# Last expert of an encoder layer: four tile squares moved among its gate and up steps, epsilon and row sums moved to ScalarE, row additions moved between VectorE's tile scalings

## The chip, the cores and the metric

The kernel runs on one core of a Trainium2 chip. The metric is the device time of one execution in microseconds (us), lower is better; the median of several runs is compared. TensorE does the matrix products, VectorE (DVE in the rows) and ScalarE (ACT) do the elementwise work, GpSimd (POOL) issues gathers and scatters and does some small arithmetic, and SyncE (SP) issues most transfers. Each engine works through its own instructions in order; a wait on a semaphore holds back everything behind it on that engine.

## The reference, cut to what matters

One encoder layer: attention of two kinds, an output projection, a mixture of 16 experts and a final norm. 1536 tokens (1024 of a prompt, 512 of a sample) of width 1024, fp32. The change touches the last expert and the final norm:

```python
def expert_choice_moe(x, w_router, w_gate, w_up, w_down):
    ...
    gate, idx = lax.top_k(aff.T, cap)          # each expert picks 128 prompt and 64 sample tokens
    xg = xt[idx]
    h = jax.nn.silu(jnp.einsum('ecd,edf->ecf', xg, w_gate)) * jnp.einsum('ecd,edf->ecf', xg, w_up)
    y = jnp.einsum('ecf,efd->ecd', h, w_down) * gate[..., None].astype(x.dtype)
    out = jnp.zeros_like(xt).at[idx.reshape(-1)].add(y.reshape(-1, D))
...
x = x + expert_choice_moe(rmsnorm(x, norm2), ...)
return rmsnorm(x, final_norm)                  # x * rsqrt(mean(x * x) + eps) * final_norm
```

## The kernel before

Experts run one after the other. For one expert, TensorE computes eight column blocks f = 0 to 7 of the gate and up products (16 pairs of matmuls each, L1969 and L1971), then two output halves c = 0 and 1 of the down product (40 matmuls each, L1988 to L1992). All weights come as fp32 and are used as two rounded parts: ScalarE makes the rounded part (`split_rounded`, L1838, two instructions for one unit) and VectorE the rest (`split_rest`, L1652, two instructions for one unit). An expert has 12 such units: 0 to 7 hold gate and up, 8 to 11 hold down. TensorE starts block f only when the units of that block are split (f = 6 needs unit 7) and when the sums of block f - 2 are out of PSUM.

ScalarE's and VectorE's work of an expert is written as steps z = 0 to 15. In steps 1 to 7 ScalarE does, in this order: `move` (copy block z - 1 of gate and up out of PSUM, L1843 and L1844), `split_rounded` of unit z + 2 (L1838), `silu` (L1861), `round_hidden` (L1865). VectorE does `sums` (L1658, L1661), `split_rest` of unit z + 2 (L1652), `hidden` (L1667) and `hidden_rest` of block z - 2 (L1674). `round_hidden` waits for `hidden`; the next `move` waits for `hidden_rest`. Unit 10 is split in step 8, unit 11 in step 10.

The final norm of the 12 row tiles (128 rows each) is woven into the last expert. After the expert before it has added its rows to x2 in DRAM, SyncE loads tiles 0 to 2 into `own_rows` (L1534) and signals them, with `final_weight`, on `final_loaded[0]`; once units 0 to 7 are split it loads tiles 3 to 10 into the free weight buffers, and once unit 9 is split, tile 11. ScalarE squares and sums each tile (`final_square`, L1870), GpSimd adds epsilon and takes the root of three tiles together (`final_roots`, L1601 and L1604), VectorE scales the tile (`final_scale`, L1714), SyncE stores it (L1549). The rows that the last expert itself changes are done apart: VectorE adds the down product to them (`finish_rows`, L1725 to L1731, one call for each output half), for which ScalarE first scales a part (`scale_output`, `y_rest`, L1851); ScalarE squares them (`row_square`, L1880), GpSimd takes their roots (L1610 to L1616), VectorE scales them (`finish_scale`, L1736), and GpSimd scatters them over the stored tiles (L1633). That scatter waits for all 12 tile stores (`final_stored`) and is the last thing the program does.

The step in which a tile is squared or scaled comes from two tables, `SQUARES_IN_STEP` and `FINAL_IN_STEP`; the order on each engine is otherwise that of the code.

Of the kernel before, what the change touches and what calls it, by code (L numbers as in the profile page):

```python
# [24 lines left out]
ALU = mybir.AluOpType  # L25
# [1303 lines left out]
def experts(p):  # L1329
# [35 lines left out]
    SQUARES_IN_STEP = {8: (0,), 9: (1, 2), 10: (3,), 11: (4, 5), 12: (6, 7), 13: (8, 9), 14: (10, 11)}  # L1365
    FINAL_IN_STEP = {9: (0,), 10: (1, 2), 11: (3, 4), 12: (5,), 13: (6, 7, 8), 14: (9, 10, 11)}
    with ExitStack() as st:
# [65 lines left out]
        final_stored = sem("final_stored")  # L1433
        base_gathered = sem("base_gathered")
# [3 lines left out]
        row_eps_added = sem("row_eps_added")  # L1438
        row_rstd = sem("row_rstd")
# [75 lines left out]
        with nc.Block() as block:  # L1515
# [37 lines left out]
            def _(pool):  # L1553
# [38 lines left out]
                pool.memset(flip[:, :], 0.0).then_inc(flip_ready, 1)  # L1592
                pool.wait_ge(flip_ready, 1)
# [4 lines left out]
                def final_roots(group):  # L1598
                    ts = slice(FINAL_GROUP * group, FINAL_GROUP * (group + 1))
                    pool.wait_ge(final_squared, ts.stop)  # L1600
                    pool.tensor_tensor(final_stats[:, 0, ts], final_stats[:, 0, ts],  # L1601
                                       p.d_eps[:, :].broadcast_to([P, FINAL_GROUP]), ALU.add).then_inc(final_eps_added, 1)
                    pool.wait_ge(final_eps_added, group + 1)
                    pool.tensor_tensor(final_stats[:, 1, ts], final_stats[:, 0, ts],  # L1604
                                       p.minus_half[:, :].broadcast_to([P, FINAL_GROUP]), ALU.pow
                                       ).then_inc(final_rstd, 1)

                def row_root(g, n):
                    pool.wait_ge(row_squared, 3 + g)
                    pool.tensor_tensor(fix_stats[0:n, g, 0:1], fix_stats[0:n, g, 0:1], p.d_eps[0:n, :], ALU.add  # L1610
                                       ).then_inc(row_eps_added, 1)
                    pool.wait_ge(row_eps_added, 2 * g + 1)
                    pool.tensor_tensor(fix_stats[0:n, g, 2:3], fix_stats[0:n, g, 0:1], fix_stats[0:n, g, 1:2], ALU.add
                                       ).then_inc(row_eps_added, 1)
                    pool.wait_ge(row_eps_added, 2 * g + 2)
                    pool.tensor_tensor(fix_stats[0:n, g, 3:4], fix_stats[0:n, g, 2:3], p.minus_half[0:n, :], ALU.pow  # L1616
                                       ).then_inc(row_rstd, 1)

                def finish():
# [8 lines left out]
                    for g, n in enumerate((CAP_P, CAP_S)):  # L1628
                        row_root(g, n)
# [16 lines left out]
            def _(dve):  # L1646
# [86 lines left out]
                def finish_scale(g):  # L1733
                    y, n = ((y_p, CAP_P), (y_s, CAP_S))[g]
                    dve.wait_ge(row_rstd, g + 1)
# [47 lines left out]
                def step(x):  # L1783
                    for z in range(16):
# [23 lines left out]
                        if z == 14 and x.is_last:  # L1808
                            finish_rows(x, 0)
                        if z == 9 and x.is_last:  # L1810
# [7 lines left out]
                    if x.is_last:  # L1818
                        finish_rows(x, 1)
                        for g in range(2):  # L1820
# [5 lines left out]
            def _(act):  # L1826
# [45 lines left out]

                def row_square(g, c):

                    cs = slice(c * 512, (c + 1) * 512)
                    y, n = ((y_p, CAP_P), (y_s, CAP_S))[g]
                    act.wait_ge(row_done, 2 * c + g + 1)
# [12 lines left out]
                def step(x):  # L1890
                    for z in range(16):
# [10 lines left out]
                        if 1 <= z <= 7:  # L1902
                            silu(x.e, z - 1)
                            round_hidden(x.e, z - 1)
# [5 lines left out]
                        if x.is_last:  # L1910
                            for t in SQUARES_IN_STEP.get(z, ()):
                                final_square(t)
                    if x.is_last:
                        for g in range(2):
                            row_square(g, 0)
                        scale_output(x, 1)
                        for g in range(2):
                            row_square(g, 1)

# [197 lines left out]
```

## Time and profile before

| | us |
|---|---|
| median of 3 runs (1816.41 to 1817.06) | 1816.84 |
| the profiled execution, its own time | 1817.82 |
| its span, in which all rows lie | 1816.0 |

The profiled execution is 0.98 us above the median. A time in a row counts from the start of the span. In a timeline row stand start, duration, engine, line, operation, what it writes and reads, the number of instructions, and in brackets the idle time before it with what ended it. SPq is the queue of transfers that SyncE issues. PEclk is the granted clock of TensorE, 1.00 for 2.4 GHz and 0.50 for 1.2 GHz.

### The profile page before, as it was taken

What the parts mean: (1) busy time and instruction counts of PE and PEld (TensorE: products, weight loads), DVE (VectorE), ACT (ScalarE), POOL (GpSimd) and SP (SyncE); (2) the same over time, 40 slices, a digit from 0 to 9 for tenths busy, and PEclk for the clock granted to TensorE, in tenths of its full rate; (3) what the DMA queues carried; (4) which work ended last, traced back from release to release, by engine and by line L of the source; (5) the groups of instructions that cost most, each with busy time, mean ns of one, the idle gap of its engine ahead of it and who ended that gap; (6) DMA issues with size and microseconds to landing.
All of it is one profiled execution on the core that took longest, in us unless ns stands there. A gap on an engine that the chain in (4) does not pass through costs nothing.

```text
span 1816.0 us, 30873 instructions
## 1 busy us (share of the span) xinstructions
PE 1716.9 (95%) x10662; PEld 1570.6 (86%) x10662; DVE 1188.6 (65%) x2313; ACT 1031.5 (57%) x2031; POOL 409.1 (23%) x563
## 2 busy tenths in 40 slices
PE   6999999899999989997599999999999999999994
PEld 6789798689999978886499999999999999999993
DVE  4442433277777864327778777787777877778776
ACT  4433333278888982111367666676666666666665
POOL 1222302244445542221101111001110011100113
PEclk9999999899999999998699999999999999999997
DMA  7455636554444744333767777777777787776784
GB/s 231 122 170 181 185 111 154 150 156 144 148 142 132 204 112 143 111 108 123 266 224 254 260 249 261 245 257 260 243 248 249 248 266 254 231 263 243 258 291 189
DMA packets 203609, 367.08 MB, mean 202 GB/s; under 512 B 39183, under 2 KB 64783, under 8 KB 202959
## 3 DMA queue, kind: packets, MB, share of 16 engines
q1 hardware_dynamic: 190268, 320.92, 52.5%
q0 software_dynamic: 13248, 44.96, 9.5%
q8 instruction: 53, 0.87, 0.2%
q14 instruction: 40, 0.33, 0.1%
HBM read 321.67 MB, written 50.45 MB: 205 GB/s over the span
## 4 chain that ended last, share of the span: by engine, by line
PE 47%; DVE 3%; ACT 1%; POOL 1%; issue 0%; DMA 0%; DVEq 0%; ACTq 0%; POOLq 0%
PE psum L1969 21%; PE psum L1971 10%; PE psum L1988 3%; PE psum L1990 3%; PE psum L1992 3%; PE psum L1989 3%; PE psum L1991 3%; DVE weight_parts L1652 1%; PE psum L1955 1%; DVE raw_weights L1714 1%; PE psum L1952 1%; ACT weight_parts L1838 0%; DVE top_at L1308 0%; DVE affT L1310 0%; ACT xT_e L1870 0%
## 5 line engine op out<-in xcount | busy, mean ns | idle before, releaser
L1969 PE MATMUL psum<-x_parts,weight_parts 128*128 128x384 f32 x2048 | 586.0, 360 | 2.0 <-DVE x_parts L1701 2.0
L1971 PE MATMUL psum<-x_parts,weight_parts 128*128 128x192 f32 x2048 | 513.8, 251 | 0.0
L1652 DVE TENSOR_TENSOR weight_parts<-raw_weights,weight_parts 128x1024 fp32r<-128x1024 f32 x384 | 451.5, 1221 | 69.5 <-ACT weight_parts L1838 69.5
L1838 ACT ACTIVATE weight_parts<-raw_weights 128x1024 fp32r<-128x1024 f32 x384 | 382.3, 1055 | 27.9 <-PE psum L1992 16.3
L1971 PEld LDWEIGHTS psum<-x_parts,weight_parts 128*128 128x128 f32 x2048 | 392.5, 192 | 0.6
L1969 PEld LDWEIGHTS psum<-x_parts,weight_parts 128*128 128x128 f32 x2048 | 385.8, 188 | 2.8 <-DVE x_parts L1701 2.2
L552 PE MATMUL psum<-x_hi,w_parts 128*128 128x512 f32 x624 | 193.9, 390 | 1.6 <-DVE kS L419 1.6
L1589 POOL DMA_INDIRECT x<-y_p,index x15 | 24.1, 1608 | 637.4 <-DVE y_s L1709 637.4
L1865 ACT ACTIVATE h_parts<-up_sum 128x192 fp32r<-128x192 f32 x128 | 46.7, 365 | 173.7 <-DVE up_sum L1667 173.7
L1143 PE MATMUL psum<-w_o_parts,mixed_parts 128*128 128x512 f32 x576 | 139.7, 399 | 4.3 <-DVE w_o_parts L1234 4.3
L779 POOL TENSOR_TENSOR logits_da<-logits_da 128x512 f32<-128x512 f32 (+1 forms) x96 | 103.8, 1103 | 171.7 <-DVE logits_da L863 171.7
L552 PEld LDWEIGHTS psum<-x_hi,w_parts 128*128 128x128 f32 x624 | 117.1, 188 | 28.9 <-issue 4.6
L1143 PEld LDWEIGHTS psum<-w_o_parts,mixed_parts 128*128 128x128 f32 x576 | 108.5, 191 | 26.9 <-issue 4.5
L552 PE MATMUL psum<-x_lo,w_parts 128*128 128x512 f32 x312 | 121.5, 389 | 0.0
L905 ACT ACTIVATE logits_da<-logits_da,stats 128x1024 f32<-128x1024 f32 (+1 forms) x96 | 96.0, 1001 | 41.0 <-DVE stats L831 40.4
L827 DVE CUSTOM_DVE_ANT_0 logits_da<-psum,bias_da 128x1024 f32<-128x1024 f32 (+1 forms) x96 | 96.9, 1044 | 33.9 <-PE psum L961 27.3
L1658 DVE TENSOR_TENSOR gate_sum<-psum,gate_sum 128x192 f32<-128x192 f32 x128 | 45.8, 358 | 103.4 <-ACT gate_sum L1843 103.4
L376 DVE TENSOR_TENSOR w_parts<-mixed,w_parts 128x2048 fp32r<-128x2048 f32 (+1 forms) x30 | 62.4, 2078 | 70.1 <-ACT w_parts L476 70.1
L329 POOL DMA_DIRECT2D q<-mixed x96 | 59.7, 628 | 200.9 <-DVE mixed L408 200.0
L1988 PE MATMUL psum<-weight_parts,h_parts 128*128 128x512 f32 x256 | 101.4, 396 | 0.3 <-DVE h_parts L1674 0.3
L1990 PE MATMUL psum<-weight_parts,h_parts 128*128 128x512 f32 x256 | 99.7, 390 | 0.0
L1992 PE MATMUL psum<-weight_parts,h_parts 128*128 128x512 f32 x256 | 99.7, 389 | 0.0
(207 smaller groups left out, 3103.5 us busy)
## 6 DMA issues: line engine op xcount, KB each, us to landing
raw_weights<-in_w_gate SPq DMA_DIRECT2D x32, 2048.0 KB, 7.8
raw_weights<-in_w_up SPq DMA_DIRECT2D x32, 2048.0 KB
raw_weights<-in_w_down SPq DMA_DIRECT2D x32, 2048.0 KB, 7.8
mixed<-in_w_in SPq DMA_DIRECT2D x96, 256.0 KB, 4.2
q_parts<-q SPq DMA_DIRECT2D x192, 128.0 KB, 3.0
bias_da<-da_rows SPq DMA_DIRECT2D x32, 512.0 KB, 4.2
q<-mixed POOLq DMA_DIRECT2D x96, 128.0 KB, 3.0
mixed<-in_x SPq DMA_DIRECT2D x12, 512.0 KB, 5.8
```

What stands on the lines that cost most here:

```text
L552: mm = pe.matmul(out, lhsT(kt), rhs(kt), start=(kt == 0 and i == 0), stop=(kt == KT - 1 and i == len(passes) - 1))
L779: pool.tensor_tensor(logits_da[:, it.slot, 0, cs], logits_da[:, it.slot, 0, cs], logits_da[:, it.slot, 1, cs], ALU.add).then_inc(combined, 1)
L827: dve.tensor_tensor_reduce(out, bank(p, 2 * m, width), bias, 1.0, -3.0e38, ALU.add, ALU.max, col(it, "max", 1, m)).then_inc(logits_ready, 1)
L905: act.activation(out, src, ACT.Exp, bias=col(it, "negmax", 1, m), accum_out=col(it, "sum", 1, m)).then_inc(exp_done, 1)
L1143: mm = pe.matmul(bank(p, 2 * i + c), mixed_parts[:, i, a, j, :], w_parts[:, b, j, c * 512:(c + 1) * 512], start=(j == 0 and k == 0), stop= ...
L1652: dve.tensor_tensor(part_half(u, 1, half), src, part_half(u, 0, half).bitcast(F32), ALU.subtract).then_inc(split, 1)
L1838: act.activation(part_half(u, 0, half), src, ACT.Copy).then_inc(rounded, 1)
L1969: pe.matmul(out.rearrange("p (h n) -> p h n", h=2), w[:, 0, k, cols], x_parts[:, k, :, :], start=(k == 0), stop=False)
L1971: mm = pe.matmul(out[:, 0:SLOTS], w[:, 1, k, cols], x_parts[:, k, 0, :], start=False, stop=(k == KT - 1))
L1988: pe.matmul(down_bank(0, c), h_hi, w_hi[:, n, :], start=first, stop=False)
L1990: pe.matmul(down_bank(0, c), h_lo, w_hi[:, n, :], start=False, stop=last)
L1992: mm = pe.matmul(down_bank(1, c), h_sample, w_lo[:, n, :], start=False, stop=last)
```

## The change

Four tiles are squared in steps 4 to 7 (`EARLY_SQUARES`), each between `silu` and `round_hidden`; the other eight follow in steps 8, 11 and 12. Tile 0 is scaled in step 7, tiles 1 and 2 in step 8, 3 to 5 in step 11, 6 to 8 in step 14, and 9 to 11 after the last `finish_rows`. The first `finish_rows` stands in step 12, ahead of tiles 6 to 8. The scaling of `final_weight` goes from step 9 to step 6. Epsilon is added by ScalarE, once for three tiles and once for the rows; the rows' two halves are summed by ScalarE too, and GpSimd takes one root for both groups of rows; it clears `fix_stats` at the start of the expert part.

```diff
-    SQUARES_IN_STEP = {8: (0,), 9: (1, 2), 10: (3,), 11: (4, 5), 12: (6, 7), 13: (8, 9), 14: (10, 11)}
-    FINAL_IN_STEP = {9: (0,), 10: (1, 2), 11: (3, 4), 12: (5,), 13: (6, 7, 8), 14: (9, 10, 11)}
+    EARLY_SQUARES = {4: (0,), 5: (1,), 6: (2,), 7: (3,)}
+    SQUARES_IN_STEP = {8: (4, 5), 11: (6, 7, 8), 12: (9, 10, 11)}
+    FINAL_IN_STEP = {7: (0,), 8: (1, 2), 11: (3, 4, 5), 14: (6, 7, 8)}
+    FINAL_AFTER = (9, 10, 11)
...
+                pool.memset(fix_stats[:, :, :], 0.0).then_inc(fix_cleared, 1)
...
-                    pool.wait_ge(final_squared, ts.stop)
-                    pool.tensor_tensor(final_stats[:, 0, ts], final_stats[:, 0, ts],
-                                       p.d_eps[:, :].broadcast_to([P, FINAL_GROUP]), ALU.add).then_inc(final_eps_added, 1)
...
+                def row_roots():
+                    pool.wait_ge(row_summed, 2)
+                    pool.tensor_tensor(fix_stats[:, :, 3], fix_stats[:, :, 2], p.minus_half[:, :].broadcast_to([P, 2]),
+                                       ALU.pow).then_inc(row_rstd, 1)
...
-                        if z == 14 and x.is_last:
+                        if z == 12 and x.is_last:
                             finish_rows(x, 0)
-                        if z == 9 and x.is_last:
+                        if z == 6 and x.is_last:
                             dve.wait_ge(final_loaded[0], 16 * 4)
...
                     if x.is_last:
                         finish_rows(x, 1)
+                        for t in FINAL_AFTER:
+                            final_scale(t)
                         for g in range(2):
                             finish_scale(g)
...
+                def add_final_eps(group):
+                    ts = slice(FINAL_GROUP * group, FINAL_GROUP * (group + 1))
+                    act.wait_ge(final_squared, ts.stop)
+                    act.activation(final_stats[:, 0, ts], final_stats[:, 0, ts], ACT.Identity, bias=p.d_eps[:, :]
+                                   ).then_inc(final_eps_added, 1)
...
                             silu(x.e, z - 1)
+                            if x.is_last:
+                                for t in EARLY_SQUARES.get(z, ()):
+                                    final_square(t)
+                                    if t % FINAL_GROUP == FINAL_GROUP - 1:
+                                        add_final_eps(t // FINAL_GROUP)
                             round_hidden(x.e, z - 1)
...
                         scale_output(x, 1)
+                        add_row_eps()
                         for g in range(2):
                             row_square(g, 1)
+                            sum_row_squares(g)
```

On ScalarE, step 4 of the last expert (the names are tiles; `own_rows` is a row tile, `h_parts` the rounded hidden block), before:

```order
L1838 ACTIVATE weight_parts<-raw_weights 128x1024 [waits gate_up,raw_loaded0]
L1838 ACTIVATE weight_parts<-raw_weights 128x1024
L1861 ACTIVATE gate_sum<-gate_sum 128x192 [waits gate_summed]
L1865 ACTIVATE h_parts<-up_sum 128x192 [waits h_done]
L1843 ACTIVATE gate_sum<-psum 128x192 [waits h_split,gate_up]
```

The same place in the change:

```order
L1835 ACTIVATE weight_parts<-raw_weights 128x1024 [waits gate_up,raw_loaded0]
L1835 ACTIVATE weight_parts<-raw_weights 128x1024
L1858 ACTIVATE gate_sum<-gate_sum 128x192 [waits gate_summed]
L1867 ACTIVATE xT_e,final_stats<-own_rows 128x1024 [waits final_loaded0]
L1862 ACTIVATE h_parts<-up_sum 128x192 [waits h_done]
L1840 ACTIVATE gate_sum<-psum 128x192 [waits h_split,gate_up]
```

The square of tile 0 with its wait for `final_loaded[0]` now stands ahead of `round_hidden` of step 4 and of the `move` of step 5.

On ScalarE, steps 8 to 14 of the last expert, before (`y_rest` is `scale_output`):

```order
L1838 ACTIVATE weight_parts<-raw_weights 128x1024 [waits gate_up,raw_loaded3]
L1838 ACTIVATE weight_parts<-raw_weights 128x1024
L1870 ACTIVATE xT_e,final_stats<-raw_weights 128x1024 [waits final_squared,final_loaded1] x3
L1870 ACTIVATE xT_e,final_stats<-raw_weights 128x1024 [waits final_squared,final_loaded2] x3
L1870 ACTIVATE xT_e,final_stats<-raw_weights 128x1024 [waits final_squared,final_loaded3]
L1851 ACTIVATE y_rest<-psum,gate 64x512 [waits y_ready_s,down]
L1870 ACTIVATE xT_e,final_stats<-raw_weights 128x1024 [waits final_squared,final_loaded3] x2
```

In the change, from unit 10 on:

```order
L1867 ACTIVATE xT_e,final_stats<-raw_weights 128x1024 [waits final_squared,final_loaded1] x2
L1873 ACTIVATE final_stats<-final_stats,d_eps 128x3 [waits final_squared]
L1835 ACTIVATE weight_parts<-raw_weights 128x1024 [waits gate_up,raw_loaded3]
L1835 ACTIVATE weight_parts<-raw_weights 128x1024
L1867 ACTIVATE xT_e,final_stats<-raw_weights 128x1024 [waits final_squared,final_loaded2] x3
L1873 ACTIVATE final_stats<-final_stats,d_eps 128x3 [waits final_squared]
L1867 ACTIVATE xT_e,final_stats<-raw_weights 128x1024 [waits final_squared,final_loaded3] x3
L1873 ACTIVATE final_stats<-final_stats,d_eps 128x3 [waits final_squared]
L1848 ACTIVATE y_rest<-psum,gate 64x512 [waits y_ready_s,down]
```

`scale_output` of half 0 now stands behind all twelve squares and three additions of epsilon.

On VectorE, the end of the program, before:

```order
L1725 SCALAR_TENSOR_TENSOR y_p<-psum,gate,rows_p 128x512 [waits down]
L1727 SCALAR_TENSOR_TENSOR y_s<-psum,gate,rows_s 64x512
L1731 TENSOR_TENSOR y_s<-y_s,y_rest 64x512 [waits y_rest_moved,sample_added]
L1736 SCALAR_TENSOR_TENSOR y_p<-y_p,fix_stats,final_weight 128x1024 [waits row_rstd]
L1736 SCALAR_TENSOR_TENSOR y_s<-y_s,fix_stats,final_weight 64x1024 [waits row_rstd]
```

In the change:

```order
L1720 SCALAR_TENSOR_TENSOR y_p<-psum,gate,rows_p 128x512 [waits down]
L1722 SCALAR_TENSOR_TENSOR y_s<-psum,gate,rows_s 64x512
L1726 TENSOR_TENSOR y_s<-y_s,y_rest 64x512 [waits y_rest_moved,sample_added]
L1709 SCALAR_TENSOR_TENSOR raw_weights<-raw_weights,final_stats,final_weight 128x1024 [waits final_rstd] x3
L1731 SCALAR_TENSOR_TENSOR y_p<-y_p,fix_stats,final_weight 128x1024 [waits row_rstd]
L1731 SCALAR_TENSOR_TENSOR y_s<-y_s,fix_stats,final_weight 64x1024 [waits row_rstd]
```

The last three tiles are scaled behind the rows' last additions, and ahead of the rows' scaling.

## Rows read from the trace of the kernel before

**Rows 1.** Page, first lines: the span, instructions

```profile
span 1816.0 us, 30873 instructions
```

**Rows 2.** Chain of work that ended last: start, duration, engine, tile, line

```profile
1800.66 0.60 POOL fix_stats L1610
...
1804.36 2.03 POOL y L1633
```

**Rows 3.** Timeline of ScalarE, steps 4 to 8 of the last expert

```profile
1754.87 0.36 ACT L1861 ACTIVATE gate_sum<-gate_sum 128x192 f32<-128x192 f32 x1
1756.73 0.36 ACT L1865 ACTIVATE h_parts<-up_sum 128x192 fp32r<-128x192 f32 x1 [1.50 <-DVE up_sum L1667]
1757.13 0.33 ACT L1843 ACTIVATE gate_sum<-psum 128x192 f32<-128x192 f32 x1
...
1766.31 0.33 ACT L1843 ACTIVATE gate_sum<-psum 128x192 f32<-128x192 f32 x1
...
1772.71 1.99 ACT L1838 ACTIVATE weight_parts<-raw_weights 128x1024 fp32r<-128x1024 f32 x2
```

**Rows 4.** Timeline of ScalarE, squares of the row tiles

```profile
1774.61 1.05 ACT L1870 ACTIVATE xT_e<-own_rows 128x1024 f32<-128x1024 f32 x1
1775.56 0.18 ACT L1870 ACTIVATION_READ_ACCUMULATOR xT_e<-own_rows 128x1 f32 x1
1775.84 1.06 ACT L1870 ACTIVATE xT_e<-own_rows 128x1024 f32<-128x1024 f32 x1
```

**Rows 5.** Load of tile 2: issue, microseconds to landing; then stretches, last columns PEclk, DMA share, GB/s

```profile
1746.24 0.48 SPq L1534 DMA_DIRECT2D own_rows<-x  x1
own_rows<-x SPq DMA_DIRECT2D x1, 512.0 KB, 14.6
1758.00:1758.50 0.50, 0.50 (x6) 0.50 (x5) 0.11 (x1) 0.50 (x1) 0.00 (x0) 1.00 0.89 352
1760.00:1760.50 0.50, 0.50 (x6) 0.50 (x5) 0.50 (x1) 0.00 (x0) 0.00 (x0) 1.00 0.04 16
```

**Rows 6.** Timeline of VectorE: split of unit 7, then the tail; then the tile stores' landing

```profile
1758.66 2.36 DVE L1652 TENSOR_TENSOR weight_parts<-raw_weights,weight_parts 128x1024 fp32r<-128x1024 f32 x2 [0.55 <-ACT weight_parts L1838]
...
1794.89 0.68 DVE L1731 TENSOR_TENSOR y_s<-y_s,y_rest 64x512 f32<-64x512 f32 x1
1795.51 3.66 DVE L1714 SCALAR_TENSOR_TENSOR raw_weights<-raw_weights,final_stats,final_weight 128x1024 f32<-128x1024 f32 x3
1799.09 0.73 DVE L1725 SCALAR_TENSOR_TENSOR y_p<-psum,gate,rows_p 128x512 f32<-128x512 f32 x1
...
1800.52 0.68 DVE L1731 TENSOR_TENSOR y_s<-y_s,y_rest 64x512 f32<-64x512 f32 x1
...
y<-raw_weights SPq DMA_DIRECT2D x9, 512.0 KB, 2.8
```

**Rows 7.** Timeline of TensorE: block 0, down product's ends, an earlier phase

```profile
1734.08 0.33 PE L1969 MATMUL psum<-x_parts,weight_parts 128*128 128x384 f32 x1
...
1770.95 0.47 PE L1988 MATMUL psum<-weight_parts,h_parts 128*128 128x512 f32 x1 [0.33 <-DVE h_parts L1674]
...
1788.98 0.39 PE L1992 MATMUL psum<-weight_parts,h_parts 128*128 128x512 f32 x1
...
680.25 19.47 PE L1143 MATMUL psum<-w_o_parts,mixed_parts 128*128 128x512 f32 x72 [4.35 <-DVE w_o_parts L1234]
```

**Rows 8.** Stretches: length, busy time of PE, PEld, DVE, ACT, POOL, then PEclk, DMA

```profile
681.00:686.00 5.00, 5.00 (x14) 3.84 (x13) 5.00 (x5) 4.40 (x5) 2.53 (x1) 0.50 1.13 220
687.00:688.00 1.00, 1.00 (x6) 0.78 (x6) 1.00 (x2) 0.96 (x1) 0.00 (x0) 1.00 1.06 414
...
889.00:894.00 5.00, 4.81 (x18) 4.81 (x19) 3.27 (x4) 1.77 (x2) 1.47 (x2) 0.50 0.63 170
894.00:895.00 1.00, 1.00 (x7) 1.00 (x6) 0.00 (x0) 0.00 (x0) 0.00 (x0) 0.72 0.76 268
236.00:238.00 2.00, 0.90 (x7) 0.90 (x8) 1.97 (x5) 0.00 (x0) 0.00 (x0) 1.00 0.10 9
```

More of the change, by code:

```diff
@@ L1433, in experts @@
         final_stored = sem("final_stored")
+        fix_cleared = sem("fix_cleared")
         base_gathered = sem("base_gathered")
@@ L1438, in experts @@
         row_eps_added = sem("row_eps_added")
+        row_summed = sem("row_summed")
         row_rstd = sem("row_rstd")
@@ L1606, in final_roots @@
                                        ).then_inc(final_rstd, 1)
[L1608 to L1617, printed above, removed]
+                def row_roots():
+                    pool.wait_ge(row_summed, 2)
+                    pool.tensor_tensor(fix_stats[:, :, 3], fix_stats[:, :, 2], p.minus_half[:, :].broadcast_to([P, 2]),
+                                       ALU.pow).then_inc(row_rstd, 1)
                 def finish():
@@ L1627, in finish @@
                         final_roots(group)
-                    for g, n in enumerate((CAP_P, CAP_S)):
-                        row_root(g, n)
+                    row_roots()
                     pool.wait_ge(final_stored, 16 * TILES)
@@ L1734, in finish_scale @@
                     y, n = ((y_p, CAP_P), (y_s, CAP_S))[g]
-                    dve.wait_ge(row_rstd, g + 1)
+                    dve.wait_ge(row_rstd, 1)
                     dve.scalar_tensor_tensor(y[:, :], y[:, :], fix_stats[0:n, g, 3:4], final_weight[0:n, :],
@@ L1871, in final_square, with add_row_eps, sum_row_squares @@
                                    ).then_inc(final_squared, 1)
+                def add_final_eps(group):
[3 more added lines that the diff above has]
+                                   ).then_inc(final_eps_added, 1)
+                def add_row_eps():
+                    act.wait_ge(row_squared, 2)
+                    act.activation(fix_stats[:, :, 0], fix_stats[:, :, 0], ACT.Identity, bias=p.d_eps[:, :]
+                                   ).then_inc(row_eps_added, 1)
+                def sum_row_squares(g):
+                    act.wait_ge(row_eps_added, 1)
+                    act.wait_ge(row_squared, 3 + g)
+                    act.activation(fix_stats[:, g, 2:3], fix_stats[:, g, 1:2], ACT.Identity, bias=fix_stats[:, g, 0:1]
+                                   ).then_inc(row_summed, 1)
                 def row_square(g, c):
@@ L1876, in row_square @@
                     y, n = ((y_p, CAP_P), (y_s, CAP_S))[g]
+                    act.wait_ge(fix_cleared, 1)
                     act.wait_ge(row_done, 2 * c + g + 1)
@@ L1912, in step @@
                                 final_square(t)
+                                if t % FINAL_GROUP == FINAL_GROUP - 1:
+                                    add_final_eps(t // FINAL_GROUP)
                     if x.is_last:
```

## The prediction

> **What bounds the kernel now.** I read the chain of work that ended last first [rows 2]: from about 1780 us on it runs through VectorE's tile scalings and row additions, then GpSimd's roots, and ends with GpSimd's scatter, which starts at 1804.36. What lies behind that start (the second scatter, its landing, the end of the program) the change leaves alone, so the question is when the scatter starts. Of the span of 1816.0 us [rows 1] the change can only touch the last expert, from 1734.08 [rows 7]. Second comes ScalarE's timeline of the gate and up steps [rows 3], because that is where the change puts new work; third the time at which that work's data arrive [rows 5]; fourth who waits for ScalarE there: VectorE [rows 6] and TensorE [rows 7, 8].
>
> TensorE's block f takes (1770.95 - 0.33 - 1734.08) / 8 = 4.57 us, some 0.02 of it drain, so 4.55 [rows 7]. ScalarE's steps come every 4.59 us (1757.13 to 1766.31 is two) [rows 3]. The two are level: nothing that holds ScalarE for more than a step stays hidden from TensorE.
>
> **The room in a step.** `silu` of step 4 starts at 1754.87 and ends at 1755.23; `round_hidden` waits 1.50 us for VectorE until 1756.73 [rows 3]. A square lasts 1.13 us, from 1774.61 to the end of its accumulator read, 1775.56 + 0.18 [rows 4]. So with its data in place an early square fits into the wait and costs nothing; the addition of epsilon in step 6 (a ScalarE instruction on 128x3, not in the trace; between the 0.18 of the accumulator read [rows 4] and the 0.36 of a 128x192 one [rows 3], I take 0.25, near the smaller form) takes the rest of it, 0.12 us at most beyond it. That was the easy half.
>
> **Its data are not in place.** Tiles 0 to 2 signal one semaphore, and the square of tile 0 waits for all. The load of tile 2 is issued at 1746.24 and lands 14.6 us later, at 1760.84, behind the last weights: the transfer engines are 0.89 busy at 1758 and at 0.04 in 1760.0 to 1760.5 [rows 5]. Before, nobody read these tiles before 1774.61 [rows 4]. Now ScalarE stands from 1755.2 to 1760.84, 5.6 us, with `round_hidden` of step 4 and the next `move` behind it. Square (1.13) and `round_hidden` (0.36) put that `move` at 1762.33 against 1757.13: 5.2 us late. Behind it in a row wait ScalarE's split of unit 7, VectorE's half of that split, `hidden` and all later steps. SyncE's loads of tiles 3 to 10 wait for unit 7 too and shift with it; the squares that read them shift as much, so that costs nothing more.
>
> **TensorE.** The split of unit 7 ended at 1758.66 + 2.36 = 1761.02 [rows 6]; now at 1766.2. Block 6 needs it and could start at 1734.08 + 6 x 4.55 = 1761.4. TensorE idles 4.8 us, where before it did not idle in these steps. After an idle of 4.35 us earlier in the program its clock was at 0.50 (1.2 GHz) from 681 to 686 and at 1.00 (2.4 GHz) from 687 [rows 7, 8]. This very pair of matmuls, at 0.50 in 889 to 894, took 4.81 / 9 = 0.534 us a pair against 4.55 / 16 = 0.284, and the low level lasted about 0.56 us into the next one [rows 8], some 10 pairs: 10 x 0.25 = 2.5 us. I take that for block 6: it ends at 1766.2 + 4.55 + 2.5 = 1773.3, and ScalarE's `move` of it starts 0.2 later, at 1773.5 against 1766.31 [rows 3]: 7.2 us late. Had the clock stayed up, it would be ScalarE's own 5.2.
>
> The page "TensorE: Matmul & The Clock Gate" of the Trainium skill, "HAM oscillation", says that a wait for data that is long enough throttles the array and the next work starts cold; Part 1 adds that the moment varies from run to run. By that rule, with which the 4.35 us gap agrees, the time is the forecast's; without it, it is that of the second rival.
>
> **The tail.** The first split of unit 10 started at 1772.71 [rows 3]. Now it is 7.2 later, and 1.1 more: VectorE scales tile 0 in step 7, ahead of the sums of block 7 for which `silu` waits (3.66 / 3 = 1.22 us [rows 6], less 0.1 in which it waited anyway). So it starts at 1781.0. Behind it ScalarE has until `y_rest`: two units, 1.90 each (1772.71 to 1774.61 [rows 3, 4]) = 3.8; eight squares of 1.23 (1774.61 to 1775.84 [rows 4]) = 9.8; three additions of epsilon = 0.75; 14.4 in all. `y_rest` starts at 1795.4, lasts 0.68, and VectorE adds it at 1796.1 instead of 1794.89 [rows 6]. Here ScalarE, not VectorE, is late, so the stall reaches the end.
> From that addition the three scalings and the next `finish_rows` follow as before: 1799.09 - 1794.89 = 4.20 gives 1800.3; the `finish_rows` itself, 1800.52 - 1799.09 + 0.62 = 2.05, ends at 1802.35; three more scalings, 3.66, end at 1806.0 [rows 6]. The last store is issued 0.1 later, lands 2.8 us after [rows 6], at 1808.9, and the scatter follows 0.2 later at 1809.1 against 1804.36: **4.7 us later**.
>
> **What costs or gives nothing.** GpSimd's row roots stood in the chain from 1800.66 until the scatter, 3.7 us [rows 2]. In the change they run beside VectorE's last three scalings, and so do ScalarE's three small additions of the rows: about 1803 to 1804.5, ahead of 1806. That is the gain meant for the tail, and it is real: without the stall all is 7.2 earlier, the scatter 2.5 us earlier than before. The rows' scalings (two of 1.28) lie beside the last store's landing. TensorE's last matmul ended at 1789.4 [rows 7] and now ends 7.2 later, at 1796.6; VectorE comes to its second half at 1800.3, so 3.7 us of cover remain. The scaling of `final_weight` (one pass over 128x1024, bounded by a tile scaling's 1.22) stands in step 6, where VectorE waits 0.55 for ScalarE's split [rows 6] and where block 6, 2.0 later than ScalarE, sets the pace. The memset of GpSimd stands at the start of the expert part, far ahead of its use.
>
> **The sum.** 1816.0 + 4.7 = 1820.7 for the span. The profiled execution was at 1817.82, 0.98 above the median; the difference lies outside what I move, so I add to the median: 1816.84 + 4.7 = **1821.5 us**.
>
> **Rivals.** (1) **The stall does not come** because tiles 0 to 2 are in place at 1755.2: the early squares are free, and 4.7 - 7.2 = -2.5 gives 1814.3, faster. It decides at once: every us that they land after 1755.2 is one us at the end, and the clock's fall adds 2 where TensorE's idle brings it about. Against it stand 14.6 us of landing and the busy engines [rows 5]; for it, nothing. 6%. (2) **The clock stays at 2.4 GHz** through the idle: 4.7 - 2.0 = 2.7, 1819.5. For it: in 236 to 238 TensorE was idle for 1.10 of 2.00 us and kept 1.00 [rows 8]. That idle is far shorter than 4.8. 12%. (3) **The landing is earlier** by up to 1.8 us, since only a trickle moves after 1759: 2.9 or more, from 1819.7. 12%. (4) **The change moves nothing at the end**, because the tail has more slack than I give it, VectorE and not ScalarE setting the `y_rest` addition: then it falls due near 1794.9 and the new order costs the three scalings behind the second `finish_rows`, minus the roots no longer in the way: within 3 us, 1818 to 1819.5. 4%.
>
> **How the numbers follow.** The forecast holds 66%. Its own spread: epsilon 0.18 to 0.36 three times, -0.2 to +0.3; the low clock as after 680.25, from there until between 686 and 687 [rows 7, 8], up to 6.7 us and thus up to 3.4 lost: +0.9; the landing, -1 to +0.5. Its own range is 1820.2 to 1822.9. The range reaches down to rivals 2 and 3: 1819.0 to 1823.0. A measurement of this kernel tells 0.2%, 3.6 us, from no change, so slower means over 1820.5. Slower: nearly all of the forecast, 65%. Same: rivals 2, 3, 4 and the forecast's lower edge, 28%. Faster: rival 1, and a little for what I do not see, 7%.
>
> **What the profile of the changed kernel would show.** ScalarE's first square at 1760.8 with an idle of over 5 us ahead of it, put down to a load; TensorE idle for some 4.8 us before a matmul of the gate and up blocks, with PEclk 0.50 for five to six us behind it; `y_rest` at about 1795.4; the last three scalings beside GpSimd's single root; the scatter at 1809, right behind the last store. The forecast is wrong if the first square starts by 1757, if no idle of TensorE stands in these steps, or if the last store lands before 1806.

## The result, and the profile of the changed kernel

The changed kernel takes 1820.93 us (median of 14 runs, 1819.06 to 1822.61), the kernel before beside it 1817.22 (14 runs, 1815.89 to 1818.91): a ratio of 1.0019 with the interval [1.0011, 1.0026], **3.7 us slower**. The forecast was 4.7 us slower, 1821.5. The profiled execution took 1820.95. Two executions among the experiments below, 5573.36 us in e7 and 4854.65 in e8, stand far outside all others and are left out of the medians and ratios.

The code ahead of the last expert is the same, but the executions do not reach it at the same moment: block 0 of the last expert starts at 1734.08 in the trace of before [rows 7] and at 1733.32 in that of after; over all traces below the moment varies from 1730.9 to 1735.0. So I count from block 0, in every kernel. The scatter started 70.28 us behind block 0 before [rows 2, 7], and 1808.43 - 1733.32 = 75.11 after it now: 4.83 later. The span ended 81.92 behind block 0 before [rows 1, 7], and ends 85.78 behind it now: 3.86 later. The second number is the one near the difference of the medians.

The page's first line, which answers to [rows 1]:

```profile
span 1819.1 us, 30877 instructions
```

Timeline of ScalarE (start, duration, engine, line, operation, and in brackets the idle time ahead with what ended it), for [rows 3, 4]:

```profile
1754.12 0.36 ACT L1858 ACTIVATE gate_sum<-gate_sum 128x192 f32<-128x192 f32 x1
1760.62 1.06 ACT L1867 ACTIVATE xT_e<-own_rows 128x1024 f32<-128x1024 f32 x1 [6.14 <-DMA own_rows<-x]
...
1761.68 0.34 ACT L1862 ACTIVATE h_parts<-up_sum 128x192 fp32r<-128x192 f32 x1
1761.93 0.31 ACT L1840 ACTIVATE gate_sum<-psum 128x192 f32<-128x192 f32 x1
...
1772.99 0.33 ACT L1840 ACTIVATE gate_sum<-psum 128x192 f32<-128x192 f32 x1 [1.94 <-PE psum L1995]
...
1794.62 0.69 ACT L1848 ACTIVATE y_rest<-psum,gate 64x512 f32<-64x512 f32 x1
```

`silu` of step 4 is over at 1754.48, and the square behind it waits 6.14 us for a load. `round_hidden` and the next `move` come out in a burst at 1761.68 and 1761.93; before, they stood at 1756.73 and 1757.13. The `move` at 1772.99 waits for TensorE, which none did in these steps before.

Timeline of TensorE and stretches of the same time (length, busy time and count of PE, PEld, DVE, ACT, POOL, then PEclk, DMA share, GB/s), for [rows 7, 8]:

```profile
1733.32 0.33 PE L1993 MATMUL psum<-x_parts,weight_parts 128*128 128x384 f32 x1
...
1765.85 0.69 PE L1993 MATMUL psum<-x_parts,weight_parts 128*128 128x384 f32 x1 [5.09 <-DVE weight_parts L1647]
```

```profile
1765.00:1770.00 5.00, 4.15 (x15) 4.15 (x16) 4.00 (x8) 4.50 (x9) 0.00 (x0) 0.50 0.60 221
1770.00:1771.00 1.00, 1.00 (x6) 1.00 (x6) 1.00 (x5) 0.83 (x4) 0.36 (x1) 0.61 0.87 344
1771.00:1773.00 2.00, 2.00 (x16) 2.00 (x15) 0.59 (x1) 0.06 (x2) 0.63 (x1) 1.00 1.02 397
```

TensorE stands for 5.09 us, where nothing stood before, and comes back at a granted clock of 0.50, its level of 1.2 GHz. Block 6 lasts from 1765.85 until the `move` behind it, 0.1 us earlier than 1772.99: about 7.03 us, against 4.55 before.

The tail: timelines of VectorE and GpSimd, and the last tile store (issue, then its landing), for [rows 2, 6]:

```profile
1795.41 0.68 DVE L1726 TENSOR_TENSOR y_s<-y_s,y_rest 64x512 f32<-64x512 f32 x1 [2.03 <-ACT y_rest L1848]
...
1801.64 3.66 DVE L1709 SCALAR_TENSOR_TENSOR raw_weights<-raw_weights,final_stats,final_weight 128x1024 f32<-128x1024 f32 x3
1805.90 1.28 DVE L1731 SCALAR_TENSOR_TENSOR y_p<-y_p,fix_stats,final_weight 128x1024 f32<-128x1024 f32 x1 [0.59 <-POOL fix_stats L1612]
1807.10 1.27 DVE L1731 SCALAR_TENSOR_TENSOR y_s<-y_s,fix_stats,final_weight 64x1024 f32<-64x1024 f32 x1
```

```profile
1802.99 2.88 POOL L1612 TENSOR_TENSOR fix_stats<-fix_stats,minus_half 128x2 f32<-128x2 f32 x1 [7.46 <-ACT fix_stats L1884]
1808.43 1.05 POOL L1628 DMA_INDIRECT y<-y_p,index  x1 [2.57 <-DVE y_s L1731]
```

```profile
1805.33 0.33 SPq L1553 DMA_DIRECT2D y<-raw_weights  x1
y<-raw_weights SPq DMA_DIRECT2D x1, 512.0 KB, 2.8
```

VectorE waits 2.03 us for `y_rest`; before, it did not. The last three scalings end at 1805.30, and the last store lands at 1805.33 + 2.8 = 1808.13. The scatter follows 0.30 later.

### The profile page after: what moved, and what is told of

The parts are those of the page before. It is cut to its first block, busy times and chain, and to the rows that moved or that the text cites. A ratio compares the mean times of both kernels' runs of the same rounds, so it can differ in the third digit from the quotient of the medians.

```text
span 1819.1 us, 30877 instructions
## 1 busy us (share of the span) xinstructions
PE 1719.0 (94%) x10662; PEld 1572.9 (86%) x10662; DVE 1188.1 (65%) x2313; ACT 1032.9 (57%) x2038; POOL 406.3 (22%) x555
## 4 chain that ended last, share of the span: by engine, by line
PE 49%; DVE 2%; ACT 1%; POOL 0%; issue 0%; DMA 0%; DVEq 0%; ACTq 0%
PE psum L1993 22%; PE psum L1995 10%; PE psum L2012 3%; PE psum L2014 3%; PE psum L2016 3%; PE psum L2013 3%; PE psum L2015 3%; PE psum L1979 1%; PE psum L1976 1%; ACT xT_e L1867 1%; DVE top_at L1308 0%; DVE affT L1310 0%; ACT weight_parts L1835 0%; DVE top L1306 0%; DMA rows_s<-xn,tokens 0%
```

## The experiments

Theory A is that of the prediction: the wait of the early square for its tile makes the stall, the stall makes TensorE's clock fall, and both reach the end through ScalarE. Theory B: the new order of the tail (rows added between the tile scalings, ScalarE's additions, one GpSimd root) costs the time. Theory C: the amount of work that ScalarE got into its gate and up steps costs it, wherever the data are. The two columns of starts and ends, and "against before", are from one trace of each kernel, counted from block 0; the medians and ratios are from runs beside the kernel before. e1 to e4 were timed beside 1816.37 (33 runs of before), e5 to e8 beside 1817.22 (30 runs). The ratios are recorded with their intervals and differ by up to 0.0003 from the plain quotient of two medians. Behind block 0 the traces of before and e2 agree within 0.01 us, but trace and medians differ by up to 1.4 us (e3: +1.64 and +3.05), so a difference smaller than that between two kernels rests on the traces alone.

| kernel | scatter starts behind block 0 | span ends behind block 0 | against before | median, ratio, interval |
|---|---|---|---|---|
| before | 70.28 | 81.92 | | |
| after | 75.11 | 85.78 | +3.86 | 1820.93, 1.0019 [1.0011, 1.0026] |
| e1 loads of own rows first | 67.66 | 78.41 | -3.51 | 1813.77, 0.9983 [0.9974, 0.9992] |
| e2 the same on before | 70.27 | 81.91 | -0.01 | 1816.43, 1.0001 [0.9992, 1.0010] |
| e3 TensorE kept busy | 72.85 | 83.56 | +1.64 | 1819.42, 1.0014 [1.0005, 1.0023] |
| e4 ScalarE's additions alone | 71.29 | 82.22 | +0.30 | 1816.99, 1.0001 [0.9992, 1.0010] |
| e5 early squares one step later | 68.46 | 79.16 | -2.76 | 1814.71, 0.9988 [0.9979, 0.9996] |
| e6 e1, `y_rest` earlier | 66.54 | 77.26 | -4.66 | 1812.09, 0.9970 [0.9958, 0.9981] |
| e7 e5, `y_rest` earlier | 66.99 | 77.67 | -4.25 | 1813.98, 0.9982 [0.9974, 0.9991] |
| e8 no early squares | 71.78 | 82.53 | +0.61 | 1817.92, 1.0003 [0.9994, 1.0012] |
| e9 e6, rows between the last tiles | 68.85 | 79.56 | -2.36 | one run each, 1815.39 beside 1816.59 |

**e1: the data in place.** On the change, SyncE issues the loads of tiles 0 to 2 ahead of the last `w_down` load, not behind it.

```diff
-                    for n, (name, half) in enumerate(LOADS):
+                    for n, (name, half) in enumerate(LOADS[:-1] if x.is_last else LOADS):
...
                 for t in range(OWN_ROWS):
                     load_final(t)
+                last = Expert(EXPERTS // 2 - 1, 1)
+                n = len(LOADS) - 1
+                name, half = LOADS[n]
+                ge(sp, split, 2 * (UNITS * last.e + LAST_UNIT[n - RAW] + 1))
+                slot = (len(LOADS) * last.i + n) % RAW
+                src = w_v[name][bass.ds(last.e, 1)].rearrange("a p k n -> p (a k) n")
+                sp.dma_start(raw[:, slot, :, :], src[:, :, half * 512:(half + 1) * 512]
+                             ).then_inc(loaded[slot], 16)
```

> The changed kernel, with one difference: SyncE issues the loads of tiles 0 to 2 and of final_weight ahead of the last expert's last 2 MB of down weights, not behind them. Theory (the early square of tile 0 waits for its load): the tiles land some 5 us earlier, near 1755.5; ScalarE's first square starts by 1755.8, TensorE does not idle in the gate and up blocks and its clock stays at 1.00; about 2.5 us faster than the kernel before (ratio near 0.9986), about 6 us faster than the change. Rival (the new order of the tail, or ScalarE's small additions, cost the time): no faster than the change, still 3 to 4 us slower than before.

The loads of the own rows now land 4.3 us behind their issue. Timelines of e1, ScalarE and VectorE:

```profile
1755.78 0.36 ACT L1866 ACTIVATE gate_sum<-gate_sum 128x192 f32<-128x192 f32 x1
1756.11 1.06 ACT L1875 ACTIVATE xT_e<-own_rows 128x1024 f32<-128x1024 f32 x1
...
1789.63 0.68 DVE L1734 TENSOR_TENSOR y_s<-y_s,y_rest 64x512 f32<-64x512 f32 x1 [2.03 <-ACT y_rest L1856]
```

The square starts at the end of `silu`, nothing waits, and TensorE does not idle in the gate and up blocks. The addition of `y_rest` comes 54.64 us behind block 0 instead of 62.09, the scatter 67.66 instead of 75.11: both 7.45 earlier, for all of the change's work is still there. Theories B and C fall: with the same order, the same instructions and the data in place, the changed kernel is 0.17% faster than the one before. VectorE waits 2.03 us for `y_rest` here too, so ScalarE is still the late one.

**e2: the same order of loads, on the kernel before.** The edit is that of e1.

> Control: the same exchange of loads in the kernel before. There the first square stands at 1774.6, after the landing at 1760.8 in any case. Theory: no change, within 0.5 us of before. Rival (the order of these loads is worth something by itself): more than 1 us faster.

Nothing: 1.0001, and the scatter at 70.27 against 70.28. What e1 gained is the wait taken away, not the loads' order.

**e3: the price of the clock.** On the change, TensorE multiplies 28 times more, into a bank that nobody reads, while it waits for unit 7. It adds work and leaves nothing out.

```diff
+                        if f == 6 and x.is_last:
+                            for i in range(28):
+                                pe.matmul(bank(p, 6, 2 * SLOTS).rearrange("p (h n) -> p h n", h=2),
+                                          x_parts[:, i % KT, 0, 0:P], x_parts[:, i % KT, :, :], start=True, stop=True)
                         if f % 2 == 0:
                             pe.wait_ge(split, 2 * (UNITS * x.e + u + 2))
```

> The changed kernel, with 28 matmuls of 384 columns into an unused PSUM bank ahead of block 6 of the last expert, where TensorE otherwise idles 5.1 us; their result is read by nobody. Theory: the idle is filled, the clock stays at 1.00 in block 6, ScalarE's move of block 6 is no longer 1.9 us late behind it, and the end comes about 2 us sooner: 1.7 us slower than before instead of 3.7. Rival (the low clock is hidden behind ScalarE): no difference from the change, 3.7 us slower than before. If the fillers outlast the wait, the gain shrinks by what they overrun.

Timelines and a stretch of e3:

```profile
1759.78 1.06 ACT L1867 ACTIVATE xT_e<-own_rows 128x1024 f32<-128x1024 f32 x1 [5.78 <-DMA own_rows<-x]
...
1760.12 5.07 PE L2026 MATMUL psum<-x_parts 128*128 128x384 f32 x28
1765.03 0.43 PE L1993 MATMUL psum<-x_parts,weight_parts 128*128 128x384 f32 x1
```

```profile
1766.00:1768.00 2.00, 2.00 (x17) 2.00 (x15) 1.43 (x3) 2.00 (x4) 0.00 (x0) 1.00 0.84 313
```

The wait of ScalarE is there as before (5.78 us), but TensorE goes on at 1.00. The `move` of block 6, which came 39.67 us behind block 0, comes 37.41 behind it (1770.25 - 1732.84), and the scatter 72.85: both 2.26 us earlier than in the change. Not all of that is the clock: in this execution the tiles landed sooner, and the first square started 26.94 us behind block 0 instead of 27.30. Block 6 started 0.34 us sooner too (32.19 against 32.53), before the clock could matter. So some 0.36 us of the 2.26 are the landing's, and 1.90 are the clock's; the change's ScalarE waited 1.94 us for TensorE at this `move`. The remaining 2.57 us (72.85 against 70.28) are the stall's own, less what the new tail gives.

The medians do not show this price as clearly: e3 is 3.05 us slower than the kernel before beside it, where 1.7 was expected, and the change 3.71, and the intervals of the two ratios overlap. The 1.90 us are read from the traces alone.

**e4: ScalarE's additions and the single root alone.** The squares, the scalings and the rows stand where they stood before; epsilon and the rows' sums are added by ScalarE.

```diff
-    EARLY_SQUARES = {4: (0,), 5: (1,), 6: (2,), 7: (3,)}
-    SQUARES_IN_STEP = {8: (4, 5), 11: (6, 7, 8), 12: (9, 10, 11)}
-    FINAL_IN_STEP = {7: (0,), 8: (1, 2), 11: (3, 4, 5), 14: (6, 7, 8)}
-    FINAL_AFTER = (9, 10, 11)
+    EARLY_SQUARES = {}
+    SQUARES_IN_STEP = {8: (0,), 9: (1, 2), 10: (3,), 11: (4, 5), 12: (6, 7), 13: (8, 9), 14: (10, 11)}
+    FINAL_IN_STEP = {9: (0,), 10: (1, 2), 11: (3, 4), 12: (5,), 13: (6, 7, 8), 14: (9, 10, 11)}
+    FINAL_AFTER = ()
...
-                        if z == 12 and x.is_last:
+                        if z == 14 and x.is_last:
                             finish_rows(x, 0)
-                        if z == 6 and x.is_last:
+                        if z == 9 and x.is_last:
```

> One part alone: ScalarE adds epsilon and the rows' sums and GpSimd takes one root for both groups of rows, with the tables and the order of the kernel before. Theory (the one root for both, 2.9 us in the trace of the change, is only free behind tile scalings): here nothing hides it, the rows' scalings start near 1805.5 instead of 1802.2, the scatter near 1807, so 2 to 3 us slower than before. Rival (fewer GpSimd instructions shorten the tail): 1 to 2 us faster than before.

It is level with before, 1.0001 [0.9992, 1.0010], where 2 to 3 us slower was expected. The end of e4, GpSimd and VectorE:

```profile
1801.82 0.70 POOL L1612 TENSOR_TENSOR fix_stats<-fix_stats,minus_half 128x2 f32<-128x2 f32 x1 [8.22 <-ACT fix_stats L1884]
1802.55 1.28 DVE L1731 SCALAR_TENSOR_TENSOR y_p<-y_p,fix_stats,final_weight 128x1024 f32<-128x1024 f32 x1 [2.00 <-POOL fix_stats L1612]
1803.76 1.27 DVE L1731 SCALAR_TENSOR_TENSOR y_s<-y_s,fix_stats,final_weight 64x1024 f32<-64x1024 f32 x1
1804.67 1.29 POOL L1628 DMA_INDIRECT y<-y_p,index  x1 [2.15 <-DVE y_p L1731]
```

The root, 2.88 us in the change, takes 0.70 here, and the scatter's issue 1.29 against 2.03 before. VectorE was idle beside the root and done early in the issue. So the row path of e4 is short enough to cost nothing, where it was expected to show. That is taken up below.

**e5: the early squares one step later**, so that the first comes when its tile has landed. The loads stay as in the change.

```diff
-    EARLY_SQUARES = {4: (0,), 5: (1,), 6: (2,), 7: (3,)}
-    SQUARES_IN_STEP = {8: (4, 5), 11: (6, 7, 8), 12: (9, 10, 11)}
-    FINAL_IN_STEP = {7: (0,), 8: (1, 2), 11: (3, 4, 5), 14: (6, 7, 8)}
+    EARLY_SQUARES = {5: (0,), 6: (1,), 7: (2,)}
+    SQUARES_IN_STEP = {8: (3, 4, 5), 11: (6, 7, 8), 12: (9, 10, 11)}
+    FINAL_IN_STEP = {8: (0, 1), 10: (2,), 11: (3, 4, 5), 14: (6, 7, 8)}
```

> The changed kernel with its early squares one step later: tiles 0, 1, 2 in steps 5, 6, 7, the other nine in steps 8, 11 and 12; tiles 0 and 1 scaled in step 8, tile 2 in step 10. The loads stand as in the change. Theory (only the wait of step 4's square for its load costs): the square of step 5 comes up near 1759.9 and waits about 1 us, most of it inside the 1.5 us that ScalarE waits there anyway; TensorE has no idle of note, its clock stays at 1.00, and the time is that of the first experiment, 2 to 3 us faster than before. Rival (early squares disturb the gate and up steps by themselves): 2 us or more slower than before.

The first square waits 1.13 us for the load instead of 6.14, starting 26.88 us behind block 0 (1761.12 - 1734.24; 27.30 in the change). TensorE does not idle in the gate and up blocks. The scatter comes at 68.46: 6.65 of e1's 7.45 us without touching a load. One step of 4.6 us was enough: the wait and the square (1.13 each) overrun the 1.50 us of room [rows 3], but the `move` behind them comes only 0.55 later than before (28.19 against 27.64 behind block 0). What e5 lacks to e1 is not that wait. Its first split of unit 10 starts earlier than e1's (39.17 against 39.61), but nine squares instead of eight stand between that split and `y_rest`, which starts at 54.65 against 53.86.

**e6: `y_rest` ahead of the last three squares**, with the edit of e1.

```diff
-                        if z == 14:
+                        if z == (12 if x.is_last else 14):
                             scale_output(x, 0)
```

> The first experiment's kernel (own rows loaded ahead of the last weights), and the first y_rest of ScalarE moved from behind the last three squares to before them (step 12). Theory (in the tail the change left VectorE waiting 2.0 us for y_rest): that wait goes, the last tile is scaled 2 us sooner and the end comes 1.5 to 2 us before the first experiment's, 4.5 to 5 us faster than before (ratio near 0.9973). Rival (something else ends last, such as the stores or the rows' root): no more than 0.5 us below the first experiment.

Timelines of e6, VectorE and GpSimd:

```profile
1781.43 3.67 DVE L1717 SCALAR_TENSOR_TENSOR raw_weights<-raw_weights,final_stats,final_weight 128x1024 f32<-128x1024 f32 x3 [0.75 <-POOL final_stats L1614]
...
1786.46 0.68 DVE L1734 TENSOR_TENSOR y_s<-y_s,y_rest 64x512 f32<-64x512 f32 x1
```

```profile
1777.26 4.14 POOL L1614 TENSOR_TENSOR final_stats<-final_stats,minus_half 128x3 f32<-128x3 f32 x1 [11.53 <-ACT final_stats L1881]
```

The wait of 2.03 us is gone. The scatter starts at 66.54, only 1.12 earlier than in e1, for a root of GpSimd took 4.14 us here and let VectorE wait 0.75 behind it (1.86 us and no wait in e1, at the same 44.3 us behind block 0). This is the fastest kernel here: 1812.09 (6 runs), **0.9970 [0.9958, 0.9981]** of the kernel before, 5.1 us faster than it and 8.8 faster than the change.

**e7: e5 and the earlier `y_rest`.** The edits of e5 and e6's, with the loads as in the change.

> Early squares from step 5 as in the fifth experiment, with the loads of the change, and y_rest ahead of the last three squares. Theory: it joins both gains without touching the loads, 3 to 4 us faster than before. Rival: as the fifth experiment.

In the trace the first square waits 0.47 us for its load, the scatter comes at 66.99 and the span ends 4.25 us earlier than before's. The median says less: 1813.98 against 1817.22, 3.2 us, 0.9982. Its interval [0.9974, 0.9991] overlaps those of e5 and e6. That e7 is slower than e6 by the 0.45 us of the traces, or by the 1.9 of the medians, is not settled.

**e8: the tail of the change without early squares.**

```diff
-    EARLY_SQUARES = {4: (0,), 5: (1,), 6: (2,), 7: (3,)}
-    SQUARES_IN_STEP = {8: (4, 5), 11: (6, 7, 8), 12: (9, 10, 11)}
-    FINAL_IN_STEP = {7: (0,), 8: (1, 2), 11: (3, 4, 5), 14: (6, 7, 8)}
+    EARLY_SQUARES = {}
+    SQUARES_IN_STEP = {8: (0, 1, 2), 11: (3, 4, 5, 6, 7, 8), 12: (9, 10, 11)}
+    FINAL_IN_STEP = {10: (0,), 11: (1, 2, 3, 4, 5), 14: (6, 7, 8)}
```

> The change without early squares: all twelve stand behind the gate and up steps (0 to 2 in step 8, 3 to 8 in step 11, 9 to 11 in step 12), tile 0 is scaled in step 10, 1 to 5 in step 11, the rest as in the change. It tells what the tail's order and ScalarE's additions are worth alone. Theory: no stall, but ScalarE reaches y_rest only after twelve squares, near 1792 on the clock of before, and VectorE waits for it; 0.5 to 2 us slower than before. Rival (the new tail order is the gain, the early squares only a price): 2 us or more faster than before.

Level with before: 1.0003 [0.9994, 1.0012], the scatter 1.5 us later, the span 0.6. VectorE waits 1.60 us for `y_rest` behind ScalarE's twelve squares. So the tail's new order by itself is no gain and no loss that can be measured. It pays when the early squares make room on ScalarE (e1, e5), and the early squares pay when their tiles are there.

**e9: the rows scaled between the last tiles**, on e6. VectorE scales tile 9, then both groups of rows, then tiles 10 and 11.

```diff
                         finish_rows(x, 1)
-                        for t in FINAL_AFTER:
-                            final_scale(t)
+                        final_scale(FINAL_AFTER[0])
                         for g in range(2):
                             finish_scale(g)
+                        for t in FINAL_AFTER[1:]:
+                            final_scale(t)
```

> The sixth experiment's kernel with the end of VectorE's work in another order: last finish_rows, tile 9, the scaling of the two groups of rows, then tiles 10 and 11. Two questions. How long GpSimd's one root of the rows takes: 2.88 us where VectorE scales tiles beside it, and it ended about 0.6 us after the last of them in the change and in five experiments, 0.70 in the fourth, where VectorE stood idle. Theory (GpSimd gets on only when VectorE lets it): here VectorE waits for the root after tile 9, and it takes 1 us or less. Rival (it is slow because of its shape or place): 2.9 us again. And what the scatter waits for, the last tile store or the rows' scaling, which end within 0.3 us of each other in the sixth: if the store, the scatter starts some 3 us after tile 11 is scaled, with both rows' scalings over 5 us done, and the end is 3 to 4 us later than in the sixth; if the scaling, right behind it, sooner than in the sixth.

Timelines of e9, GpSimd and VectorE, and its last store:

```profile
1794.28 0.70 POOL L1620 TENSOR_TENSOR fix_stats<-fix_stats,minus_half 128x2 f32<-128x2 f32 x1 [2.60 <-ACT fix_stats L1893]
...
1802.89 1.05 POOL L1636 DMA_INDIRECT y<-y_p,index  x1 [7.92 <-DMA y<-raw_weights]
```

```profile
1797.40 2.47 DVE L1717 SCALAR_TENSOR_TENSOR raw_weights<-raw_weights,final_stats,final_weight 128x1024 f32<-128x1024 f32 x2
```

```profile
1799.90 0.33 SPq L1561 DMA_DIRECT2D y<-raw_weights  x1
y<-raw_weights SPq DMA_DIRECT2D x1, 512.0 KB, 2.7
```

The rows are scaled by 1797.48, and the scatter waits for the last store, which lands at 1802.6: 0.29 before it. It was to be 3 to 4 us later than e6 and is 2.31 later. VectorE's last tile scaling ends 2.41 later (65.83 against 63.42 behind block 0): the order costs the two scalings of 1.2 and a wait of 0.81, some 3.3 in all, and 0.87 came back because this time the root at 44.3 us behind block 0 took 1.86 us and not 4.14. So the row roots and row scalings really lie beside the tile scalings and the store, as the change has them, and in e9 the store binds the end. e9 was run once.

## Why the prediction was right, point by point

The mechanism came as forecast up to the last store; two things behind it, the row root and the issue of the scatter, did not. The time is nearer than the sum deserves: 1821.5 against 1820.93 is 0.6 us, made of a loss forecast 1.0 too large (4.7 against 3.7) and a kernel before that was 0.38 slower in these runs than the 1816.84 taken as base.

Microseconds behind block 0. Those of the forecast are its times less 1734.08, those of after less 1733.32.

| step | forecast | measured |
|---|---|---|
| first early square starts | 26.8 | 27.30 |
| `move` of step 5 | 28.25 | 28.61 |
| TensorE's idle | 4.8 long | 5.09 long |
| block 6 starts | 32.1 | 32.53 |
| block 6 lasts | 4.55 + 2.5 | 7.03 |
| `move` of block 6 | 39.4 | 39.67 |
| first split of unit 10 | 46.9 | 47.06 |
| `y_rest` starts | 61.3 | 61.30 |
| last tile scaled | 71.9 | 71.98 |
| row root ends | 70.4 | 72.55 |
| last store lands | 74.8 | 74.81 |
| scatter starts | 75.0 | 75.11 |
| span ends | 86.6 | 85.78 |

The agreement at `y_rest` to some hundredths is luck in part: block 6 started 0.4 later than forecast, and smaller terms behind it came out shorter.

**The stall.** ScalarE waited 6.14 us where 5.6 was forecast: tile 2 landed half a microsecond later, counted from block 0. The reading that decided the case, a load issued at 1746.24 that needs 14.6 us, and the transfer engines busy behind the weights [rows 5], held. Rivals 1 and 3 (the tiles in place, or there 1.8 us sooner) fell with this row. What tile 0 to 2 would be worth if they were in place, 7.2 us by the first rival, e1 measured as 7.45. Rival 1's "faster than before", with 2.5 us, was 2.62 at the scatter in e1.

**The clock.** The clock stood at 0.50 from the restart at 1765.85 and came back between 1770 and 1771, after about 5 us; in the stretches that the prediction drew on it was low from 889 to about 0.56 us past 894 [rows 8]. Block 6 took 2.48 us more, where 2.5 was forecast. As TensorE's block, and not ScalarE's step, set the pace behind it, only part of this reached the end: 2.0 by the forecast, 1.90 by e3 once the earlier landing is taken off its 2.26. Rival 2 (the clock stays up) is what e3 builds; it forecast 2.7 us later than before at the scatter, and e3 has 2.57 (2.93 with the landing of the change). The page "TensorE: Matmul & The Clock Gate" of the Trainium skill, section "HAM oscillation", says that the work behind a long wait for data starts cold: the trace agrees, with 0.50 behind 5.09 us of idle and, in e3, 1.00 where the same wait was filled.

**The tail's start.** ScalarE, not VectorE, was late at `y_rest`, to a tenth of a microsecond; rival 4 fell. The additions of epsilon last 0.30, but the next instruction starts 0.20 behind the first (1784.69, 1784.89), 0.21 behind the second and 0.32 behind the third: 0.73 in all, where the sum had 0.75. From the split of unit 10 to `y_rest` it is 14.24 us (1780.38 to 1794.62) against 14.4.

**The row root was mis-sized.** The prediction had the roots done by 1804.5, "ahead of 1806", and called that the gain meant for the tail. ScalarE's sum came in time (the root started at 1802.99), but the root took 2.88 us, as long as VectorE scaled tiles. It ended at 1805.87, 0.57 behind the last scaling, and VectorE waited 0.59 for it. This cost nothing: the rows' scalings ended at 1808.37, and the last store, which the scatter needs too, landed at 1808.13, 0.30 before the scatter started. How near these two are is seen there; the profile names the scaling, which ended 0.06 before the scatter, as what released it. In e9 the rows' scalings were long done, the profile names the store, and the scatter again started 0.29 behind its landing. That speaks for the store in the change as well, though only e9 shows it apart.

**The step that failed**, and made the loss 1.0 us too large, is a sentence of the first part: "What lies behind that start (the second scatter, its landing, the end of the program) the change leaves alone". It did not. In the kernel before the scatter of `y_p` started while VectorE scaled `y_s`, a row of before that the prediction did not use:

```profile
1804.17 1.28 DVE L1736 SCALAR_TENSOR_TENSOR y_s<-y_s,fix_stats,final_weight 64x1024 f32<-64x1024 f32 x1 [0.70 <-POOL fix_stats L1616]
```

The scatter's issue took 2.03 us and ended 0.94 behind this scaling, at 1806.39. In the change the scaling is over when the scatter starts, and the issue takes 1.05. That is 0.98 us that the forecast left out, and with it nearly all of its error (4.83 - 0.98 = 3.85): from the scatter's end to the end of the span it is 1816.0 - 1806.39 = 9.61 before and 1819.1 - 1809.48 = 9.62 after. With the term in it the sum is 4.7 - 1.0 = 3.7 us, which is what the medians show. The prediction's word "slower" (65%) meant more than 0.2%, and was said of a number 1 us further out. The measured change lies on that edge: 0.20% by the medians, 0.19% by the ratio, whose interval [1.0011, 1.0026] holds the edge. It is slower beyond the noise, but not settled as more than 0.2%.

**What the new work gives.** The prediction put the change without its stall 2.5 us ahead of before at the scatter. Piece by piece: the tail and the additions alone are worth nothing (e4 +0.30, e8 +0.61 us), the early squares with their data in place make it -3.51 (e1), and `y_rest` ahead of the last squares -4.66 (e6).

## What to carry to other kernels

Work that is put into a wait of an engine needs its own data there by then: look up when the load lands, not when it is issued, and count what stands behind the new wait on that engine. A load that nobody has read early may sit behind large ones, and moving the first reader one step later can be worth nearly as much as moving the load. Where one engine is freed of a piece of work at the end, look at what else runs beside each GpSimd instruction there, before and after, since its length can hang on VectorE.

## What the runs showed of the hardware that was not expected

**GpSimd's small instructions, and the issue of its DMAs, stretch while VectorE works on two tensors in SBUF.** The root of 128x2 took 0.70 us with VectorE idle (e4, e9) and 2.88 beside its tile scalings (after, e1, e3, e5 to e8). Roots of 128x3 took 0.85 to 0.90 at best and up to 4.14. In the long ones the end lies behind the end of VectorE's row of work by a little less than a root alone takes: 0.57 in the change (1805.30, 1805.87), 0.71 in e6 (VectorE until 1780.69, root until 1781.40). The scatter's issue took 1.05 with VectorE idle, 1.29 in e4, where 0.36 us of a scaling were left, and 2.03 before, where 1.09 were left; behind VectorE's end it is 0.93 and 0.94. The page "GPSIMD Engine Reference" of the Trainium skill, section "Specifications", says that GpSimd shares its SBUF interfaces with VectorE and that instructions with two SBUF inputs contend; the scalings and splits have two, and these rows agree. The change's own trace also has the other case. Its third root of tiles began beside scalings and ended behind them:

```profile
1790.82 1.96 POOL L1606 TENSOR_TENSOR final_stats<-final_stats,minus_half 128x3 f32<-128x3 f32 x1 [3.89 <-ACT final_stats L1873]
```

```profile
1788.40 3.67 DVE L1709 SCALAR_TENSOR_TENSOR raw_weights<-raw_weights,final_stats,final_weight 128x1024 f32<-128x1024 f32 x3
1791.99 0.74 DVE L1720 SCALAR_TENSOR_TENSOR y_p<-psum,gate,rows_p 128x512 f32<-128x512 f32 x1
```

The root ended at 1792.78, 0.71 us behind the last scaling (1792.07), though VectorE went on with `y_p` and then `y_s` in that time; these instructions take one of their two tensors from PSUM, and GpSimd got on beside them. In e6 (1791.44, 1790.73), e7 (1791.69, 1790.98) and e9 (1791.68, 1790.97) a root ended 0.71 behind the last scaling too, with the same instructions on VectorE.

**It is not the same each time.** The root at 44.3 us behind block 0 stands beside the same VectorE work in e1, e6 and e9, and took 1.86, 4.14 and 1.86 us. What lets it in between two of VectorE's instructions in one execution and not in the other, no run here shows.
